# Two attention mixers of a decoder trunk: score products of two heads side by side, the causal mask on VectorE, another order at the seam between them, and output products moved ahead of a norm

## The chip, the cores and the metric

The kernel runs on one core of one Trainium2 chip. The metric is the device time of one execution in microseconds (us). The engines are TensorE (PE; PEld is its weight load), VectorE (DVE), ScalarE (ACT), GpSimd (POOL) and SyncE (SP, which issues most of the DMA). Each engine runs its own instructions in program order; semaphores tie the engines together.

## The reference, cut to what matters

The program computes two layers of a trunk with 512 positions and a width of 1024. In each layer one input projection feeds four token mixers, each 256 wide; one output product joins them, and a mixture of 32 experts follows.

```python
for l in range(DEPTH):                       # DEPTH = 2
    proj = rmsnorm(x, norm1_g[l]) @ w_in[l]
    pa, pb, pc, pd = jnp.split(proj, cut, axis=-1)
    out_a = moba_attention(...)              # 4 heads of 64, causal
    out_b = rwkv7_time_mix(pb, ...)          # linear recurrence, 4 heads of 64
    out_c = sgu_mix(...)                     # chunked gating
    out_d = diff_attention(...)              # 4 heads, two softmax maps of width 32 each
    mixed = jnp.concatenate([out_a, out_b, out_c, out_d], axis=-1)
    x = x + mixed @ w_out[l]
    x = x + hier_moe(rmsnorm(x, norm2_g[l]), ...)
return rmsnorm(x, final_g)

# in attention A, per head and block of 128 queries: s = q k^T, masked causally, then
p = jax.nn.softmax(s, axis=-1);  out = p @ v
# in attention D:
attn = p[:, :, 0] - lam * p[:, :, 1]         # of two softmax maps
o = rmsnorm(attn @ v, subln_g) * (1.0 - lambda_init)
```

With 512 positions every query block of A sees all past key blocks, so A is plain causal attention here. All numbers are 32-bit floats; each matrix product of the program leaves two MATMUL records in the trace, a transpose leaves one.

## The kernel before, in words

A layer has an input part (norm, projection), the mixers, the output product, the routing, and the expert part, where 32 experts' weights stream from HBM. The change is in the mixers and in the output product.

`mixer_steps()` writes out by hand the order of the mixers' steps; each engine runs the same list through `run_mixers` and skips what isn't its own. So an engine does its share of a step only after its share of all earlier steps. The steps that matter here:

- `("attn", (m, u))`, m = A or D: step u of an attention's pipeline over 16 units. A unit is one block of 128 queries of one head; A goes from the block with 1 key block (width 128) to the one with 4 (width 512), D from 512 down to 128. At step u PE makes the scores of unit u (L818, then L820, which adds the causal mask as a transposed product of a constant), transposes the probabilities of unit u-2 (L830), and multiplies those of unit u-3 with the values (L842). DVE takes the row maximum (L1538) of the scores in PSUM; for D it also joins the two maps (L1548, L1550, L1552). ACT copies the finished outputs of unit u-4 (L1222), then the transposed probabilities of unit u-2 (L1231), then takes the exponentials of unit u (L1239), in this order. L842 writes one bank only, so it waits for ACT's copy of the unit before (L1222). A head of A has 64 channels, a map of a head of D has 32: scores of neighbouring heads (A) or of the two maps (D) take different rows of the array. The scores rotate through four PSUM banks (3, 4, 5, 6).
- `("rwkv", (c, m, step))`: the recurrence in four chunks, for two pairs of heads c. Each chunk has parts Z (L733, L735), B (L741) and S (L748 to L758), each waiting on copies by ACT or DVE of the part before; chunk 3 leaves out L748 and L749. These parts are put between the attention units of A, by the table `UNITS_PER_PART`. F1, F2 and F3 (L762, L765, L770) and G (DVE only, L1525 and L1526) are the norm and gate behind it; they stand between steps of D.
- `("turn_qk", "D")` (L799): turns queries and keys of D; it stands near the end of A.
- `turns(j)` (L848) turns the outputs of A and of the gating mixer; `early_out` (L867) starts the output product of the first column half for two row blocks out of them, before D is done.

After the last step of D, PE makes four more output products each for row blocks 2 and 3 (L916), then waits for `mixed_done`: DVE squares, sums and scales D's outputs (L1561 to L1571) behind the last unit of D. Then PE turns D's outputs (L848) and the recurrence's scales (L898), and goes through the rest of the products, first column half, then second (L916). SP's queue holds loads of expert weights that wait for marks in this order: parts B and S of chunk 3, `mixed_done`, the output sums.

## Time and profile before

| | us |
|---|---|
| median of 3 runs | 1835.2 (1834.05 to 1835.56) |
| the profiled execution's own time | 1835.94 |
| its span, from first to last instruction | 1834.1 |
| mean granted TensorE clock | 0.962 |

| engine | busy us | share of the span |
|---|---|---|
| PE | 1622.2 | 88% |
| DVE | 576.0 | 31% |
| ACT | 286.3 | 16% |
| POOL | 158.9 | 9% |

The mixers with attention stand twice in the span, from about 237 to 352 us and from about 1140 to 1255 us; the output product follows each. From about 450 to 860 us and again in the second half the DMA engines are over 90% busy with expert weights. A row of the timeline gives the start, the length, the engine, line, operation and tile, the count of records it merges, and in brackets how long the engine was idle before it and what released it. Records of PE overlap, so the time that a group of products takes is read from its start to the next group's start. PEclk is the granted TensorE clock, where 1.00 is 2.4 GHz and 0.50 is 1.2 GHz.

### The profile page before, as it was taken

The page shows a single profiled execution, that of the slowest core. Times are in us where ns is not written, and L with a number is a line of the kernel's source. Part 1 is how long each engine was busy: PE and PEld are TensorE (multiplying, and loading weights), DVE is VectorE, ACT ScalarE, POOL GpSimd, SP SyncE. Part 2 cuts the span into 40 slices and gives each one's busy share as a digit, 9 for nine tenths or more (in the row PEclk, how much of TensorE's full clock was granted, in tenths as well). Part 3 has the DMA queues.
Part 4 walks back from the last instruction along what each step waited for, and adds up shares of the span by engine and source line. Part 5 has one row for each costly group of instructions (what it writes and reads, how often), then busy time and mean ns, then how long its engine had stood idle before and what let it go on. Part 6 is the DMA issues. An engine that isn't in the chain of part 4 may idle for free.

```text
span 1834.1 us, 22309 instructions
## 1 busy us (share of the span) xinstructions
PE 1622.2 (88%) x9240; PEld 989.8 (54%) x9240; DVE 576.0 (31%) x1282; ACT 286.3 (16%) x694; POOL 158.9 (9%) x175
## 2 busy tenths in 40 slices
PE   7999999998999788787799999989989987888773
PEld 3445776657565455444444557755665654545441
DVE  2174324625221111221422742264342211112115
ACT  3131144311000000000123212442200000000001
POOL 0010000002211011110000100000022111011000
PEclk9999997899999999999899999979999999999997
DMA  9212013149999999999821111214489999999994
GB/s 321 92 44 66 1 47 138 39 181 363 412 425 422 424 424 424 423 423 421 362 107 76 52 58 46 79 60 166 166 360 420 424 423 424 424 424 422 423 418 188
DMA packets 72712, 486.58 MB, mean 265 GB/s; under 512 B 24413, under 2 KB 26397, under 8 KB 37792
## 3 DMA queue, kind: packets, MB, share of 16 engines
q1 hardware_dynamic: 62240, 468.81, 62.3%
q0 software_dynamic: 10368, 16.30, 2.4%
q8 instruction: 76, 1.25, 0.3%
q14 instruction: 28, 0.23, 0.0%
HBM read 472.24 MB, written 30.21 MB: 274 GB/s over the span
## 4 chain that ended last, share of the span: by engine, by line
PE 62%; DMA 25%; DVE 5%; SPq 4%; issue 3%; ACT 1%; POOL 1%; DVEq 0%; POOLq 0%; ACTq 0%
PE banks L963 12%; PE banks L623 12%; DMA RING<-in_w_up 7%; PE banks L978 6%; PE banks L612 6%; DMA RING<-in_w_down 5%; PE banks L916 5%; DMA TOK<-in_w_up 4%; DMA RING<-in_w_gate 3%; PE banks L818 3%; DMA TOK<-in_w_gate 2%; PE banks L842 2%; SPq L493 2%; PE banks L941 2%; SPq L495 2%
## 5 line engine op out<-in xcount | busy, mean ns | idle before, releaser
L963 PE MATMUL banks<-RING,XS 128*64 128x256 f32 x2752 | 320.2, 389 | 50.2 <-DMA RING<-in_w_up 28.4
L963 PEld LDWEIGHTS banks<-RING,XS 128*64 128x64 f32 x2752 | 224.2, 140 | 157.3 <-issue 46.0
L623 PE MATMUL banks<-RING,XNT 128*128 128x512 f32 x512 | 224.3, 595 | 0.6 <-DMA RING<-in_w_in_blocks 0.6
L978 PE MATMUL banks<-RING,XS 128*64 128x512 f32 x768 | 178.8, 606 | 28.5 <-issue 15.5
L1794 DVE SCALAR_TENSOR_TENSOR XS<-banks,TABLE,XS 128x256 f32<-128x256 f32 x58 | 28.1, 484 | 447.0 <-PE banks L963 447.0
L623 PEld LDWEIGHTS banks<-RING,XNT 128*128 128x128 f32 x512 | 96.7, 191 | 117.9 <-issue 116.7
L1272 ACT ACTIVATE XS<-banks,TABLE 128x256 f32<-128x256 f32 x58 | 27.5, 474 | 791.6 <-PE banks L963 791.6
L978 PEld LDWEIGHTS banks<-RING,XS 128*64 128x64 f32 x768 | 61.6, 138 | 112.5 <-issue 112.5
L2012 POOL DMA_INDIRECT y_rows<-XS,SOLVE x64 | 64.5, 1007 | 543.0 <-DVE XS L1836 520.6
L612 PE MATMUL banks<-XNT,RING 128*128 128x512 f32 x256 | 110.2, 592 | 0.0
L1836 DVE COPY XS<-banks 128x512 f32<-128x512 f32 x64 | 44.3, 691 | 204.8 <-PE banks L978 192.0
L963 PE MATMUL banks<-TOK,XS 128*64 128x256 f32 x832 | 94.4, 380 | 13.0 <-DMA TOK<-in_w_gate 7.0
L916 PE MATMUL banks<-RING 128*128 128x512 f32 x224 | 100.2, 601 | 0.1
L963 PEld LDWEIGHTS banks<-TOK,XS 128*64 128x64 f32 x832 | 67.4, 137 | 43.6 <-issue 11.5
L612 PEld LDWEIGHTS banks<-XNT,RING 128*128 128x128 f32 x256 | 48.6, 190 | 61.2 <-issue 61.2
L1538 DVE TENSOR_REDUCE SMALL<-banks 128x1 f32<-128x128 f32 (+3 forms) x96 | 44.2, 488 | 107.8 <-PE banks L820 107.4
L916 PEld LDWEIGHTS banks<-RING 128*128 128x128 f32 x224 | 42.0, 193 | 48.0 <-issue 47.7
L818 PE MATMUL banks<-XNT 32*128 32x512 f32 (+7 forms) x192 | 61.5, 590 | 0.0
L842 PE MATMUL banks<-TOK,RING 128*128 128x64 f32 x320 | 51.3, 300 | 8.9 <-ACT TOK L1222 8.7
L842 PEld LDWEIGHTS banks<-TOK,RING 128*128 128x128 f32 x320 | 48.5, 223 | 14.0 <-issue 13.6
L969 PE MATMUL banks<-CF,XS 128*128 128x128 f32 x132 | 30.1, 310 | 25.6 <-DVE XS L1794 18.4
L1239 ACT ACTIVATE XNT<-banks,SMALL 128x128 f32<-128x128 f32 (+3 forms) x96 | 49.8, 526 | 14.0 <-DVE SMALL L1538 13.7
(335 smaller groups left out, 1783.7 us busy)
## 6 DMA issues: line engine op xcount, KB each, us to landing
RING<-in_w_down SPq DMA_DIRECT2D x46, 2048.0 KB, 27.0
RING<-in_w_up SPq DMA_DIRECT2D x44, 2048.0 KB, 28.4
RING<-in_w_gate SPq DMA_DIRECT2D x42, 2048.0 KB, 26.7
RING<-in_w_in_blocks SPq DMA_DIRECT2D x12, 2048.0 KB, 9.6
TOK<-in_w_gate SPq DMA_DIRECT2D x12, 2048.0 KB, 35.5
TOK<-in_w_up SPq DMA_DIRECT2D x10, 2048.0 KB, 32.4
XNT<-in_w_down SPq DMA_DIRECT2D x8, 2048.0 KB, 30.5
TOK<-in_w_down SPq DMA_DIRECT2D x6, 2048.0 KB, 30.9
```

Source lines behind the costliest of these rows:

```text
L493: sp.dma_start(dst, src.rearrange("a p n -> p (a n)")).then_inc(full, 16)
L612: last = mm(bank[:, :], w[:, k, j * P:(j + 1) * P], XNT[:, k, :], start=(k == 0), stop=(k == KD - 1))
L623: last = mm(bank[:, :], XNT[:, k, i * P:(i + 1) * P], w[:, k, :], start=(k == 0), stop=(k == KD - 1))
L818: mm(banks[a][:, 0:w], QKT[rows, h // 2, i * P:w], QKT[rows, 2 + h // 2, 0:w], start=True, stop=False)
L842: last = mm(PS[0][:, 0:HD], PT[:, n % 2, b * P:(b + 1) * P], VAD[:, b, v0:v0 + HD], start=(b == 0), stop=(b == i))
L916: last = mm(PS[SUM_BANK[n][i]][:, :], src[:, i * P:(i + 1) * P], w[:, k, :], start=(k == 0), stop=(k == (KD - 1 if n else 3)))
L963: last = mm(bank[f * CAP:(f + 1) * CAP, 0:256], rows[:, k, :], w[:, k, f * 256:(f + 1) * 256], start=(k == 0), stop=(k == KD - 1))
L978: last = mm(PS[5][n * CAP:(n + 1) * CAP, :], HT[:, j, f * CAP:(f + 1) * CAP], w[:, k, n * BN:(n + 1) * BN], start=(k == 0), stop=(k == KF ...
L1239: ac(PB[:, u % 2, a, 0:w], PS[SCORE_BANKS[k % 4]][:, 0:w], ACT.Exp, bias=nmx[:, base + n:base + n + 1], accum_out=sums[:, base + n:base + ...
L1538: V.tensor_reduce(nmx[:, base + n:base + n + 1], PS[SCORE_BANKS[k % 4]][:, 0:w], AX.X, ALU.max, negate=True).then_inc(s["maxed"], 1)
L1836: V.tensor_copy(YS[h], PS[5][:, :]).then_inc(y2_copied, 1)
L2012: pool.indirect_dma_start(y_halves, bass.IndirectOffsetOnAxis(ap=YROW[:, e:e + 1], axis=0), YS[h], None, bounds_check=4 * SEQ - 1, oob_is_ ...
```

## The change

Five things are edited, all within the mixers and the output product.

1. Scores of A are issued in pairs: at every even step PE issues those of two neighbouring heads behind each other (rows 0 to 63 and 64 to 127 of the array), at odd steps none. L820 goes for A; in its place DVE adds the mask to the block of the unit in PSUM, by one more instruction per unit ahead of the maximum, chained by a semaphore.
2. `UNITS_PER_PART` spreads the 16 units over the parts of chunks 0 to 2. Chunk 3 (Z, B, S) moves behind D's steps 0, 1 and 2. F1 and F2 stand one pair of heads at a time behind D's steps 3 to 6; F3 and G stand behind step 7 (before: 5 and 6); the four `turns` behind steps 7 and 8 (before: 9 and 11).
3. A's steps 17 and 18 now both stand ahead of D's step 0 (before: 17, D's 0, 18, 19).
4. `early_out` does one product at a time, behind D's steps 10 to 17 (before two at a time behind 14 to 17).
5. Four products of the second column half for row block 0 are made ahead of the wait for `mixed_done`, into bank 4. The recurrence's scales, turned into banks 4 and 7 before, go to banks 7 and 5; the second waits for DVE's first copy out of bank 5.

On PE at the start of attention A in layer 0, before (L799 turns A's queries and keys, L733 is Z, L741 is B of chunk 0):

```order
L799 MATMUL banks<-CF,TOK 128x128 x16
L733 MATMUL banks<-RING 128x64 x4
L818 MATMUL banks<-XNT 128x128
L820 MATMUL banks<-CF 128x128
L818 MATMUL banks<-XNT 128x128
L820 MATMUL banks<-CF 128x128
L741 MATMUL banks<-RING,X 128x64 x4
L818 MATMUL banks<-XNT 128x128
L820 MATMUL banks<-CF 128x128
L830 MATMUL banks<-CF,XNT 128x128
```

and after (L793, L727, L807, L735, L829 and L841 are the lines L799, L733, L818, L741, L830 and L842 of before):

```order
L793 MATMUL banks<-CF,TOK 128x128 x16
L727 MATMUL banks<-RING 128x64 x4
L807 MATMUL banks<-XNT 128x128 x2
L735 MATMUL banks<-RING,X 128x64 x4
L807 MATMUL banks<-XNT 128x128 x2
L829 MATMUL banks<-CF,XNT 128x128 x2
L841 MATMUL banks<-TOK,RING 128x64
```

Two scores stand in a row, and no mask product behind them.

On PE at the seam between the two attentions, before (L799 turns D's queries and keys; L818 and L820 are now D's scores and masks):

```order
L799 MATMUL banks<-CF,TOK 128x128 x16
L830 MATMUL banks<-CF,XNT 128x128 x4
L842 MATMUL banks<-TOK,RING 128x64 x4
L818 MATMUL banks<-XNT 128x512 x2
L820 MATMUL banks<-CF 128x128 x2
L842 MATMUL banks<-TOK,RING 128x64 x4
L818 MATMUL banks<-XNT 128x512 x2
L820 MATMUL banks<-CF 128x128 x2
L818 MATMUL banks<-XNT 128x512 x2
L820 MATMUL banks<-CF 128x128 x2
L830 MATMUL banks<-CF,XNT 128x128 x4
```

and after:

```order
L793 MATMUL banks<-CF,TOK 128x128 x16
L829 MATMUL banks<-CF,XNT 128x128 x4
L841 MATMUL banks<-TOK,RING 128x64 x8
L817 MATMUL banks<-XNT 128x512 x2
L819 MATMUL banks<-CF 128x128 x2
L727 MATMUL banks<-RING 128x64 x2
L729 MATMUL banks<-RING,SCAN 128x128
L727 MATMUL banks<-RING 128x64 x2
L729 MATMUL banks<-RING,SCAN 128x128
L817 MATMUL banks<-XNT 128x512 x2
L819 MATMUL banks<-CF 128x128 x2
L735 MATMUL banks<-RING,X 128x64 x4
```

A's last product with the values stands ahead of D's first scores, and Z and B of chunk 3 stand between D's scores.

On PE behind D's last unit, before:

```order
L842 MATMUL banks<-TOK,RING 128x64
L916 MATMUL banks<-RING 128x512 x8
L848 MATMUL banks<-CF,TOK 128x128 x8
L898 MATMUL banks<-CF,SCAN 128x128 x8
L916 MATMUL banks<-RING 128x512 x28
```

and after:

```order
L841 MATMUL banks<-TOK,RING 128x64
L917 MATMUL banks<-RING 128x512 x12
L847 MATMUL banks<-CF,TOK 128x128 x8
L899 MATMUL banks<-CF,SCAN 128x128 x8
L917 MATMUL banks<-RING 128x512 x24
```

Four of the output products (L916, L917) have moved ahead of the turns of D's outputs.

The diff, cut to its core:

```diff
-UNITS_PER_PART = [2, 1, 2, 1, 2, 2, 1, 2, 2, 1, 1]
+UNITS_PER_PART = [2, 2, 1, 2, 2, 2, 2, 2, 1]
...
-            for ch in range(4):
+            for ch in range(3):
                 for n, part in enumerate("ZBS"):
                     yield from both(part, ch)
...
-            second = ([("attn", ("A", 16)), ("turn_qk", "D"), ("attn", ("A", 17)), ("attn", ("D", 0)), ("attn", ("A", 18)), ("attn", ("A", 19))])
+            yield from [("attn", ("A", 16)), ("turn_qk", "D"), ("attn", ("A", 17)), ("attn", ("A", 18)), ("attn", ("D", 0))]
+            yield from both("Z", 3)
+            yield "attn", ("A", 19)
+            one = lambda c, *step: [("rwkv", (c, SCANS[c][1], step))]
+            beside = {1: both("B", 3), 2: both("S", 3), 3: one(0, "F", 1), 4: one(1, "F", 1), 5: one(0, "F", 2), 6: one(1, "F", 2),
+                      7: both("F", 3) + both("G") + [("turns", (0,))], 8: [("turns", (j,)) for j in range(1, 4)]}
+            for n, step in enumerate((i, k) for i in range(2) for k in (0, 1, 4, 5)):
+                beside[10 + n] = [("early_out", step)]
             for u in range(1, 20):
                 yield "attn", ("D", u)
...
+                yield from beside.get(u, [])
...
+                        if u < 16 and m == "A" and u % 2 == 0:
+                            i, h = unit_of[m][u]
+                            w = (i + 1) * P
+                            for a in range(2):
+                                k = 4 + u + a
+                                wait_bank(k)
+                                rows = slice(a * 64, a * 64 + 64)
+                                mm(score_bank(k)[:, 0:w], QKT[rows, h // 2, i * P:w], QKT[rows, 2 + h // 2, 0:w], start=True, stop=True).then_inc(s["scores"], 1)
+                        elif u < 16 and m == "D":
...
-                    for n, ks in ((0, (0, 1, 4, 5)), (0, (6, 7)), (0, (2, 3)), (1, range(KD))):
+                    early, late = (0, 1, 4, 5), (2, 3, 6, 7)
+                    for n, ks in ((0, early), (1, early), (0, (6, 7)), (0, (2, 3)), (1, range(KD))):
...
+                                if c:
+                                    pe.wait_ge(*at(layer, mt_v, 1))
                                 for ch in range(4):
-                                    last = tr(PS[(4, 7)[c]][:, ch * P:(ch + 1) * P], FIN[c][1][:, ch * P:(ch + 1) * P], ident)
+                                    last = tr(PS[(7, 5)[c]][:, ch * P:(ch + 1) * P], FIN[c][1][:, ch * P:(ch + 1) * P], ident)
...
-                        for i in (2, 3) if n == 0 and ks[0] == 0 else range(NT):
+                        for i in ((2, 3), (0,))[n] if ks is early else range(NT):
...
-                            for k in ks:
+                            for k in late if n and i == 0 and ks is not early else ks:
...
+                                if m == "A":
+                                    own = PS[SCORE_BANKS[k % 4]][:, i * P:w]
+                                    link(V.scalar_tensor_tensor(own, later, NEG, own, ALU.mult, ALU.add))
```

## Rows read from the trace of the kernel before

**Rows 1.** Windows: A and D of layer 0, D of layer 1, a stretch behind it.

```profile
core 0: us, PE busy (x) PEld busy (x) DVE busy (x) ACT busy (x) POOL busy (x), PEclk, DMA share, GB/s
237.20:287.12 49.92, 48.99 (x355) 37.53 (x353) 14.41 (x50) 27.08 (x85) 1.87 (x3) 1.00 0.22 85
287.12:351.98 64.86, 61.25 (x281) 40.06 (x281) 36.64 (x94) 30.46 (x103) 0.00 (x0) 0.74 0.14 59
1189.56:1254.85 65.29, 58.99 (x281) 38.67 (x281) 36.54 (x94) 30.77 (x103) 0.00 (x0) 0.79 0.14 59
1264.15:1270.00 5.85, 5.85 (x22) 3.83 (x23) 4.44 (x8) 0.00 (x0) 0.00 (x0) 0.71 0.80 308
```

**Rows 2.** Timeline of PE: a score of width 128, then A's step 15.

```profile
238.20 0.48 PE L818 MATMUL banks<-XNT 64*128 64x128 f32 x2
238.62 0.33 PE L820 MATMUL banks<-CF 128*128 128x128 f32 x1
...
275.89 1.12 PE L818 MATMUL banks<-XNT 64*128 64x512 f32 x2
276.95 0.33 PE L820 MATMUL banks<-CF 128*128 128x128 f32 x1
277.11 0.60 PE L830 MATMUL banks<-CF,XNT 128*128 128x128 f32 x4
277.55 1.00 PE L842 MATMUL banks<-TOK,RING 128*128 128x64 f32 x8
278.39 1.06 PE L741 MATMUL banks<-RING,X 128*128 128x64 f32 x8
```

**Rows 3.** Products on changing rows of the array: D's first scores, then the chunks' products.

```profile
287.12 1.13 PE L818 MATMUL banks<-XNT 32*128 32x512 f32 x4
...
L678 PE MATMUL banks<-SCAN x32: 376/376/480, 131.2 to 140.1; 64*128 64x256 f32 x32
```

**Rows 4.** DVE and ACT, groups by form: a 128x128 operation on PSUM, and what ends a unit.

```profile
L1456 DVE SCALAR_TENSOR_TENSOR TOK<-banks,PCOL,TOK 128x128 f32<-128x128 f32 x8 | 2.8, 351 | 3.0 <-PE banks L656 2.8
L1538 DVE TENSOR_REDUCE SMALL<-banks 128x1 f32<-128x512 f32 x12 | 7.9, 688 | 21.9 <-PE banks L820 21.9
L1239 ACT ACTIVATE XNT<-banks,SMALL 128x512 f32<-128x512 f32 x12 | 8.2, 684 | 5.6 <-DVE SMALL L1538 5.6
L1222 ACT ACTIVATE TOK<-banks,SMALL 128x64 f32<-128x64 f32 x32 | 10.1, 316 | 3.7 <-PE banks L842 3.7
```

**Rows 5.** Timeline of PE at the seam, layer 0.

```profile
282.14 1.07 PE L842 MATMUL banks<-TOK,RING 128*128 128x64 f32 x8 [0.23 <-ACT TOK L1222]
286.11 1.08 PE L842 MATMUL banks<-TOK,RING 128*128 128x64 f32 x8 [0.70 <-ACT TOK L1222]
291.06 1.94 PE L842 MATMUL banks<-TOK,RING 128*128 128x64 f32 x8 [2.45 <-ACT TOK L1222]
```

**Rows 6.** Windows over part Z and parts B, S of chunk 3, layer 0.

```profile
274.41:275.89 1.48, 1.48 (x14) 1.36 (x13) 0.00 (x0) 1.13 (x4) 0.00 (x0) 1.00 0.00 0
278.39:281.31 2.92, 2.92 (x30) 2.38 (x30) 0.65 (x3) 0.90 (x3) 0.00 (x0) 1.00 0.22 43
```

**Rows 7.** Windows where the clock falls or rises in D of layer 0.

```profile
288.00:290.00 2.00, 0.61 (x4) 0.20 (x2) 1.29 (x2) 0.73 (x3) 0.00 (x0) 0.81 0.97 418
...
306.00:308.00 2.00, 2.00 (x8) 0.58 (x7) 1.92 (x4) 0.63 (x1) 0.00 (x0) 0.92 0.00 0
316.00:318.00 2.00, 2.00 (x10) 0.91 (x10) 0.17 (x1) 0.00 (x0) 0.00 (x0) 0.64 0.00 0
332.00:334.00 2.00, 2.00 (x11) 1.70 (x12) 0.00 (x0) 1.15 (x4) 0.00 (x0) 0.59 0.00 0
```

**Rows 8.** Timelines of layer 1 around G: one of its four on DVE, then PE.

```profile
1223.10 0.75 DVE L1525 SCALAR_TENSOR_TENSOR RING<-RING,PCOL,XS 128x512 f32<-128x512 f32 x1
...
1226.78 0.55 PE L830 MATMUL banks<-CF,XNT 128*128 128x128 f32 x3 [2.83 <-DVE XNT L1552]
```

**Rows 9.** Timeline of PE behind D, layer 0.

```profile
351.98 7.09 PE L916 MATMUL banks<-RING 128*128 128x512 f32 x16
361.29 1.09 PE L848 MATMUL banks<-CF,TOK 128*128 128x128 f32 x8 [2.22 <-DVEq L1572]
```

More of the change, by code:

```diff
@@ L333, in mixer_steps @@
             first = [("attn", ("A", u)) for u in range(16)]
[L334 removed]
+            for ch in range(3):
                 for n, part in enumerate("ZBS"):
                     yield from both(part, ch)
[L337 to L343 removed]
+                    for _ in range(UNITS_PER_PART[3 * ch + n]):
+                        yield first.pop(0)
+            yield from [("attn", ("A", 16)), ("turn_qk", "D"), ("attn", ("A", 17)), ("attn", ("A", 18)), ("attn", ("D", 0))]
[6 more added lines that the diff above has]
+                beside[10 + n] = [("early_out", step)]
             for u in range(1, 20):
                 yield "attn", ("D", u)
[L346 to L355 removed]
+                yield from beside.get(u, [])
         def run_mixers(**do):
@@ L859, in turns, with early_out @@
                         turn_outputs(j, 1 + j % 2, src, t)
-                    def early_out(i, part):
-                        if part == 0:
+                    def early_out(i, k):
+                        if k == 0:
                             pe.wait_ge(*at(layer, mt_a, 4))
@@ L916, in _ @@
                                 last = mm(PS[SUM_BANK[n][i]][:, :], src[:, i * P:(i + 1) * P], w[:, k, :], start=(k == 0), stop=(k == (KD - 1 if n else 3)))
-                            if ks[-1] == (KD - 1 if n else 3):
+                            if ks is not early and ks[-1] == (KD - 1 if n else 3):
                                 last.then_inc(res_ps, 1)
@@ L1526, in rwkv @@
                             link(V.scalar_tensor_tensor(FIN[c][0], FIN[c][0], pc("lnb", c), gate, ALU.add, ALU.mult))
+                    later = CFs[:, CF["unit"][0]:CF["unit"][0] + P]
                     def attn(m, u):
```

31 lines of the change are left out of this document (5 added, 26 removed).

## The prediction

> **What bounds the kernel now.** I read the windows over the two attentions first, because every edit lies between 237 and 364 us of layer 0 and between 1140 and 1267 us of layer 1. In A (49.92 us in layer 0; layer 1 runs the same instructions and I take it as equal) PE is busy 48.99 us at a clock of 1.00, ACT 27.1 and DVE 14.4: PE bounds it, and what leaves PE shortens it [rows 1]. In D (64.86 and 65.29 us) PE is busy 61.25 and 58.99 us, but at a mean clock of 0.74 and 0.79, so about half of the time runs at 1.2 GHz; DVE is busy 36.6 us, ACT 30.5 [rows 1]. The timeline of PE gives the idle places: 0.23, 0.70 and 2.45 us at the seam, each ended by ACT's copy of outputs [rows 5], 2.83 us behind G in layer 1 [rows 8], and 2.22 us ahead of D's turned outputs [rows 9]. The windows of two microseconds show the clock falling at 289 us, behind the last of the seam's waits, and at 316 us, and coming back at 306 and 332 us [rows 7]. All of this is PE or what PE waits for. The DMA is busy 0.14 of D [rows 1]: the expert weights are loaded when marks of the mixers and of the output product are reached, so I take a shift of the mixers' end to arrive whole at the end of the span.
>
> **Part 1, pairs in A.** A single score of 64 rows takes 0.42 us from its start to L820's at width 128 and 1.06 at width 512 [rows 2]; 0.63 and 0.84 for the widths between are my estimate from the straight line. Do two on different rows run together? Both maps of D's first unit, four records of width 512, take 1.13 us with their end, the two records of one head of A 1.12 [rows 3, 2]. And 64 records of 64x256, L678 and L679 on alternating halves, of which the row of L678 stands for half, fill 131.2 to about 140.4 us: 0.144 us for one, against 0.31 by A's 0.63 for two [rows 3]. So a pair costs as much as one. Of four heads at each width two disappear: 2 x (0.42 + 0.63 + 0.84 + 1.06) = 5.9 us. L820 costs 0.16 us to the next start [rows 2], 16 times that 2.6. Together PE loses 8.5 us per layer. DVE gets 16 mask instructions of 0.35 us [rows 4], 5.6 us onto 14.4 in 50: hidden as a sum, but it lengthens the chain behind each score. At width 512 that chain is mask 0.35, maximum 0.69, exponential 0.68, output copy 0.32 [rows 4] and four handovers that I take at 0.1: 2.4 us until L842 of the next step may start. Between them PE has only some 1.7 us (turn 0.44, values 0.84, turn 0.44 [rows 2]) where an even and the following odd step stand together. The new table puts a chunk's part there in most places; where it doesn't or where the part is short (steps 2 and 3, 5, 7, 13) I count 0.8, 0.7, 0.2 and 0.2, so 1.9 us per layer. Bounds: 0, and 8 pairs x 1.2 = 9.6 us. I take 1.9 since PE waits nowhere in A now except at its end.
>
> The Trainium skill, TensorEngine Tiling (Array Packing), section Performance Considerations, warns that tiling speeds up TensorE but not the evacuation of PSUM, which may then bound. By this rule the paired stage would run at its readers' pace; it is the rival called readers below.
>
> **Part 2, the seam and chunk 3.** Z, B and S of chunk 3 (1.48 + 2.92 = 4.4 us [rows 6]) leave A and enter D. A's last product, 0.84 us [rows 2], now precedes D's scores. The 2.45 us wait came from ACT's order: the copy that frees L842's bank stood behind D's first two exponentials, and these behind scores and maxima. With A's step 18 ahead of D's step 0 it stands behind one copy; 0.5 us are left, somewhat more than L1222's own 0.32 [rows 4, 5]. The waits of 0.23 and 0.70 stay, the first growing to 0.7, because S no longer stands ahead of step 16. In D's steps 0 to 2 the chunk's parts lie where PE otherwise had only scores; for DVE's queue there I count 0.5 us. The parts B and S also release SP's reload of x and two weight loads later; the queue behind them is idle for tens of microseconds, so nothing.
>
> A, start to D's first score: 49.92 - 8.5 - 4.4 + 0.84 - 0.93 (idle of before) + 0.7 + 0.7 + 0.5 + 1.9 = 40.7 us, a gain of 9.2.
>
> **Part 3, D.** At full clock D's PE work is its busy time less half of what ran at 1.2 GHz. Layer 0: 64.86 x 0.26 x 2 = 33.7 us slow, 1.4 of them idle, so 61.25 - 16.2 = 45.1. Layer 1: 65.29 x 0.21 x 2 = 27.4, so 58.99 - 13.7 = 45.3 [rows 1]. After: 45.2 - 0.84 + 4.4 = 48.8 us. Waits: DVE piles up at F1 (about 2 us of DVE beside each of steps 3 and 4, with maxima and joining of about 2.6 against PE's 3.5): 1.6 us in sum over steps 4 to 6. Turns and G: G is four DVE instructions of 0.75 [rows 8], now directly behind F3. `turns` 3 waits for ACT's copy of `turns` 1, which stands in ACT's queue behind the exponentials of unit 8, which wait for maxima queued behind G: 3.1 + 0.4 + 1.1 + 0.6 = 5.2 us against 3.2 us of PE work in between, so 2.0 us, in place of the 2.83 that layer 1 had [rows 8]. First wait on F3's last DVE step: 0.4. With the 0.5 of part 2 that is 4.5. D without any slow clock: 53.3 us.
>
> **Part 4, the clock.** Before, it cost 16.2 and 13.7 us of PE's work (part 3). It fell behind the 2.45 us wait, behind the thin products of F3 in layer 0, behind the 2.83 us wait in layer 1, and each time stayed low for 13 to 17 us, until L762, a dense product of all rows, or L848 came [rows 7]. After, the first wait is gone, but F3 and the 2 us at `turns` 3 follow each other closely, so I expect a fall there in both layers, ended earlier because `early_out` (dense, full rows) starts at step 10: some 7 us low, 3 us lost. A fall at the seam remains possible in about one of three layers, at 6 us. Taken: 5 us per layer; bounds 0 and 16. D is then 58.3 us, a gain of 6.6 and 7.0.
>
> **Part 5, output products ahead of the norm.** PE works 7.09 us after its last unit and waits 2.22 [rows 9]. Four products are 8 records of 7.09 / 16 = 0.44: 3.5 us. They cover the 2.22 and are taken from later, where PE has no idle time; the gain is 2.22 per layer, and D's outputs are turned 1.3 us later relative to DVE, which the products behind them (7.1 us ahead of the first use of the recurrence's part) hide. The new wait on DVE's first copy ends when PE has turned the first scales, 1.3 us after the start: 0 to 0.3 us, taken 0, since the second copy is waited for anyway. In layer 1 the clock fell behind this wait: mean 0.71 over 5.85 us [rows 1], 5.85 x 0.29 = 1.7 us. Sum 2.2 x 2 + 1.7 = 6.1 us.
>
> **Sum.** 2 x 9.2 + 6.6 + 7.0 + 6.1 = 38.1 us. The profiled execution took 1835.9 us, 0.7 above the median; 1835.9 - 38.1 = 1797.8, or 1797 on the scale of the median.
>
> **Rivals.**
> - *No falls of the clock in D.* The seam's long wait is gone, and chunk 3 fills D's start. Against it: F3 and the wait at `turns` 3. 2 x 5 less: 1787 us.
> - *The clock is low as long as before.* D's scores, turns and narrow products kept it low for 13 to 17 us even with PE 100% busy [rows 7]; one fall at the seam and one at F3 give it again. 15 us per layer instead of 5, of which some 3 per layer return because waits on DVE and ACT disappear at half speed: + 14, 1811 us.
> - *Readers.* ACT and DVE set the pace of A: 9.6 instead of 1.9 us of waits per layer, + 15: 1812 us. Against it speak ACT's 27 and DVE's 20 us under PE's 37. The rule of the Trainium skill named above would have it so; the sums say no, the local chains partly yes.
> - *Pairs don't run together.* 5.9 us per layer stay on PE, of which it hides the 1.9 of waits: + 8, 1805 us. Against it: rows 3.
> - *Slower.* A now runs at 1.00 throughout because it has no gaps. With waits in it and less PE work the clock could fall early and stay down, as it did in D with PE 100% busy. 37 us of A's work at 1.2 GHz cost 37 less 3.8 of waits, 33 per layer: 1797 + 66 = 1863 us. It outweighs the gain once more than about 19 us of A's work per layer, half of it, run at half clock.
>
> **How the numbers follow.** Forecast 0.50, no falls 0.18, clock as before 0.17, readers 0.07, pairs 0.03, slower 0.03, and 0.02 for something that leaves the time as it is. The forecast case alone spans clock costs of 2 to 9 us and other waits of +-3 us per layer: 1785 to 1811. The range takes in the no-falls case with a few microseconds fewer waits, 1779, and the middle cases up to 1815. A measurement of this kernel can tell about 0.2% from no change. Faster by more than that 0.95, within it 0.02, slower 0.03.
>
> **What would show it.** In the profile after: A from its first score part to D's first score 40 to 42 us at clock 1.00; two L807 per pair in the time of one; PE's wait ahead of D's step 0 under 1 us; a wait of about 2 us ahead of the last three turns (L847), at D's step 8, with the clock falling near it; no wait ahead of D's turned outputs; D 54 to 63 us. The forecast is wrong if the clock in A is under 1.00, if waits in A sum to over 5 us, or if the weights' loads start no earlier although the mixers end earlier.

## The result and the profile after

The changed kernel takes 1824.4 us (median of 14 executions, 1809.1 to 1836.7) against 1834.7 us (14 executions, 1829.4 to 1844.9) of the kernel before on the same chip. The ratio is 0.993 (95%: 0.991 to 0.9951), some 13 us faster. The forecast was 1797 us, with 1815 as the upper end: the sign was right, the size was not. A ratio is formed without executions over 1.5% above the fastest of their kernel, so it can stand below the ratio of the medians (by the medians the change is worth 10 us, and the ratio given for e1 rests on two of its six executions).

The changed kernel was measured twice more without any edit: e1 was profiled in one of its longest executions, e13 in its shortest. Together with the first they are the key to this case, so all three are read here. First, the page of the changed kernel (span, busy time of PE, then busy tenths and granted clock in 40 slices of the span):

```profile
span 1811.6 us, 22279 instructions
...
PE 1602.1 (88%) x9208; PEld 978.8 (54%) x9208; DVE 583.2 (32%) x1314; ACT 286.3 (16%) x694; POOL 158.8 (9%) x175
...
PE   7999999999799888777799999999998997988773
...
PEclk9999997999999999999999999979999999999997
```

This profiled execution took 1813.4 us, 11 below the median. The only slices with a clock under nine tenths, apart from the last, are those of D in layer 0 and layer 1. The windows over A (from its first score part to D's first score) and D (from there to the first output product behind it), layer 0 and then layer 1; columns as in [rows 1]:

```profile
237.22:281.14 43.92, 39.09 (x306) 31.07 (x304) 17.80 (x64) 26.22 (x82) 1.86 (x3) 0.99 0.09 38
281.14:344.87 63.73, 62.37 (x314) 40.03 (x313) 36.95 (x96) 31.35 (x106) 0.00 (x0) 0.79 0.25 99
1129.90:1175.23 45.33, 40.66 (x307) 32.63 (x305) 17.80 (x64) 26.54 (x82) 1.86 (x3) 0.95 0.09 37
1175.23:1239.04 63.81, 62.50 (x314) 40.07 (x313) 36.95 (x96) 31.40 (x106) 0.00 (x0) 0.79 0.26 99
```

Against [rows 1], A has lost 6.0 and 4.6 us and D only 1.1 and 1.5. The clock of D is 0.79, where the forecast had it low for some 7 us. A isn't at 1.00 in either layer, which the prediction had named as a sign of being wrong: the clock is low for its last microsecond, and in layer 1 also for 3.4 us from 1167.6 us.

The timeline of PE shows that the pairs run as meant (L807), and which waits A now has (L841 is the product with the values, L1223 ACT's copy of its outputs, L793 the turning of D's queries and keys):

```profile
238.23 0.49 PE L807 MATMUL banks<-XNT 64*128 64x128 f32 x4
238.65 1.10 PE L735 MATMUL banks<-RING,X 128*128 128x64 f32 x8
...
261.52 1.13 PE L807 MATMUL banks<-XNT 64*128 64x512 f32 x4
...
271.62 1.08 PE L841 MATMUL banks<-TOK,RING 128*128 128x64 f32 x8 [0.23 <-ACT TOK L1223]
272.53 0.61 PE L829 MATMUL banks<-CF,XNT 128*128 128x128 f32 x4
274.14 1.08 PE L841 MATMUL banks<-TOK,RING 128*128 128x64 f32 x8 [1.00 <-ACT TOK L1223]
...
278.11 1.08 PE L841 MATMUL banks<-TOK,RING 128*128 128x64 f32 x8 [0.70 <-ACT TOK L1223]
279.68 1.53 PE L841 MATMUL banks<-TOK,RING 128*128 128x64 f32 x8 [0.50 <-ACT TOK L1223]
281.14 2.08 PE L817 MATMUL banks<-XNT 32*128 32x512 f32 x4
```

Two scores of width 512 take 1.13 us, where one took 1.12 [rows 2]. The wait of 2.45 us behind D's first scores [rows 5] is gone; A's last product with the values, now ahead of these scores, waits 0.50 us. The last row is the point of this document: D's first scores take 2.08 us, against 1.13 in [rows 3]. The clock has fallen at the seam all the same, without the long wait. It fell at 280.1 us, within the last L841, which is why that row takes 1.53 us where the others take 1.08.

Now e13, the same program, in the same four stretches:

```profile
237.22:280.68 43.46, 38.64 (x306) 30.66 (x304) 17.80 (x64) 26.20 (x82) 1.86 (x3) 1.00 0.09 39
280.68:336.13 55.45, 53.41 (x313) 34.63 (x313) 36.76 (x96) 31.15 (x106) 0.00 (x0) 0.94 0.30 114
1120.62:1164.63 44.01, 39.19 (x307) 31.15 (x305) 17.80 (x64) 26.20 (x82) 1.86 (x3) 0.99 0.09 39
1164.63:1226.97 62.34, 60.48 (x313) 38.92 (x313) 36.88 (x96) 31.34 (x106) 0.00 (x0) 0.82 0.27 102
```

And the same stretch of its PE:

```profile
278.11 1.08 PE L841 MATMUL banks<-TOK,RING 128*128 128x64 f32 x8 [0.70 <-ACT TOK L1223]
279.68 1.08 PE L841 MATMUL banks<-TOK,RING 128*128 128x64 f32 x8 [0.50 <-ACT TOK L1223]
280.68 1.13 PE L817 MATMUL banks<-XNT 32*128 32x512 f32 x4
```

The rows ahead of the seam agree with those above to 0.01 us, waits included; in one execution the last L841 takes 1.53 us, in the other 1.08. And e1, the first 58 us of D in both layers:

```profile
281.36:339.36 58.00, 57.65 (x206) 37.92 (x207) 26.82 (x58) 20.44 (x59) 0.00 (x0) 0.50 0.28 109
1185.96:1243.96 58.00, 57.65 (x206) 37.92 (x207) 26.83 (x58) 20.44 (x59) 0.00 (x0) 0.50 0.28 109
```

PE is busy 57.65 of 58 us, and runs at 1.2 GHz throughout. The lengths of A and D account for the whole difference between the executions of the changed kernel:

| trace | A, layers 0 and 1 | D, layers 0 and 1 | sum | its execution |
|---|---|---|---|---|
| before | 49.92, 49.92 | 64.86, 65.29 | 230.0 | 1835.9 |
| changed | 43.92, 45.33 | 63.73, 63.81 | 216.8 | 1813.4 |
| changed, e1 | 43.45, 43.46 | 76.86, 76.83 | 240.6 | 1836.6 |
| changed, e13 | 43.46, 44.01 | 55.45, 62.34 | 205.3 | 1801.9 |
| forecast | 40.7, 40.7 | 58.3, 58.3 | 198.0 | 1797.8 |

From the second row to the third the sum rises by 23.8 us and the time by 23.2; to the fourth it falls by 11.5 and the time by 11.5. The changed kernel's time varies with that of D, and D's with the time for which the clock stays low.

Between the profiled executions of before and after lie 22.5 us: 13.2 from A and D, 6.2 from part 5 (below), and 3.1 from elsewhere; outside the mixers the clock of this execution was low for some 41 us in sum, before for 51.

### The profile page after: what moved, and what is told of

The parts are those of the page before. It is cut to its first block, busy times and chain, and to the rows that moved or that the text cites. A ratio compares the mean times of both kernels' runs of the same rounds, so it can differ in the third digit from the quotient of the medians.

```text
span 1811.6 us, 22279 instructions
## 1 busy us (share of the span) xinstructions
PE 1602.1 (88%) x9208; PEld 978.8 (54%) x9208; DVE 583.2 (32%) x1314; ACT 286.3 (16%) x694; POOL 158.8 (9%) x175
## 4 chain that ended last, share of the span: by engine, by line
PE 62%; DMA 26%; DVE 4%; issue 3%; SPq 3%; ACT 1%; POOL 1%; DVEq 0%; POOLq 0%; ACTq 0%
PE banks L617 12%; PE banks L964 11%; PE banks L606 6%; DMA TOK<-in_w_up 6%; PE banks L979 6%; PE banks L917 5%; DMA RING<-in_w_up 5%; DMA RING<-in_w_gate 3%; DMA RING<-in_w_down 3%; DMA TOK<-in_w_gate 2%; DMA SCAN<-in_w_up 2%; PE banks L841 2%; SPq L487 2%; PE banks L942 2%; PE banks L817 2%
## 5 line engine op out<-in xcount | busy, mean ns | idle before, releaser
L964 PEld LDWEIGHTS banks<-RING,XS 128*64 128x64 f32 x2752 | 220.8, 139 | 157.9 <-issue 43.1
L979 PEld LDWEIGHTS banks<-RING,XS 128*64 128x64 f32 x768 | 61.1, 138 | 111.6 <-issue 111.6
L917 PE MATMUL banks<-RING 128*128 128x512 f32 x224 | 99.1, 595 | 0.0
L917 PEld LDWEIGHTS banks<-RING 128*128 128x128 f32 x224 | 41.5, 190 | 47.1 <-issue 46.9
L841 PE MATMUL banks<-TOK,RING 128*128 128x64 f32 x320 | 48.7, 287 | 9.8 <-ACT TOK L1223 9.4
L841 PEld LDWEIGHTS banks<-TOK,RING 128*128 128x128 f32 x320 | 44.7, 207 | 16.3 <-issue 15.1
L1136 ACT ACTIVATE TOK<-banks 128x512 f32<-128x512 f32 x32 | 19.2, 599 | 203.8 <-PE banks L617 203.8
L1986 POOL DMA_INDIRECT XS<-x_rows,SOLVE x32 | 33.8, 1058 | 191.6 <-PE banks L957 189.3
```

Source lines behind the costliest of these rows:

```text
L841: last = mm(PS[0][:, 0:HD], PT[:, n % 2, b * P:(b + 1) * P], VAD[:, b, v0:v0 + HD], start=(b == 0), stop=(b == i))
L917: last = mm(PS[SUM_BANK[n][i]][:, :], src[:, i * P:(i + 1) * P], w[:, k, :], start=(k == 0), stop=(k == (KD - 1 if n else 3)))
L964: last = mm(bank[f * CAP:(f + 1) * CAP, 0:256], rows[:, k, :], w[:, k, f * 256:(f + 1) * 256], start=(k == 0), stop=(k == KD - 1))
L979: last = mm(PS[5][n * CAP:(n + 1) * CAP, :], HT[:, j, f * CAP:(f + 1) * CAP], w[:, k, n * BN:(n + 1) * BN], start=(k == 0), stop=(k == KF ...
```

## The experiments

**Where the loss is: e1, the changed kernel again (no edit).**

> The changed kernel once more, unchanged, for a second trace and for the spread of its times. Theory 'clock': the changed kernel's time differs between executions by how much of it runs at 1.2 GHz; over the executions the time falls as the mean granted clock rises, by about 1.5 to 2 us for each 0.001 of the clock, and a trace of a slower execution (over 1820 us) shows low stretches inside attention A that the first trace (1813 us) has only in layer 1. Rival 'loads': the spread comes from the expert weights' loads; then the mixers of a slower execution take what those of the first trace take (A 43.9 and 45.3 us, D 63.7 and 63.8 us) and the difference lies between 450 and 860 us or behind 1380 us.

Measured: 1834.4 us (1805.7 to 1839.1, 6 executions), ratio 0.9881 (0.982 to 0.9941); the kernel before beside it has the same median, 1834.2. The mean clock of an execution goes with its time: 0.966 at 1805.7 us, 0.949 at 1836.6. The trace is the one shown above: low at the seam, and low for 58 us. The loads are not the cause, as A and D hold the whole difference to the first trace. But the low stretches were expected inside A, and there the clock is 1.00 in both layers: they lie in D.

**The waits at the seam filled: e2.** Five dense products of all rows, 256 wide, stand where PE waits in A's steps 16 to 18. Nothing reads what they write.

```diff
+                    def fill(n):
+                        for _ in range(n):
+                            mm(PS[1][:, 0:2 * P], cst("head"), CFs[:, CF["unit"][0]:CF["unit"][0] + 2 * P], start=True, stop=True)
...
+                        if m == "A" and u in {16: 2, 17: 2, 18: 1}:
+                            if u == 16:
+                                pe.wait_ge(*at(layer, mix["A"]["s_done"], 3))
+                            fill({16: 2, 17: 2, 18: 1}[u])
```

> The changed kernel with five dense products of width 256 on all rows (constants, results unused, about 0.44 us each) put into PE's three waits at the seam: two ahead of the value products of A's step 16, two at step 17, one at step 18. Theory 'clock': the fall at the seam, 23 to 24 us low in both layers, is what ate the gain; with the waits filled the clock stays at 1.00 through D's first steps in at least one layer, D shrinks from 63.7 to some 52 us there, and the time falls by 8 to 20 us against the changed kernel. Rival 'narrow products': the clock falls because of what PE computes at the seam and in D's start (32 rows, turns, narrow products), not because of the waits; then it falls a few microseconds later anyway and the time stays within 4 us of the changed kernel's.

Measured: 1807.2 us (1797.5 to 1814.4, 6), ratio 0.9838 (0.9799 to 0.9877), the kernel before on that chip 1834.2. Added work makes the kernel some 15 us faster: it is 27 below the kernel before, where the changed kernel was 10 and 13 below in its two larger sets of executions. A is as long as before the edit, 43.47 us. The timeline of PE in e2 (L798 fills, L821 is D's score, L849 the product with the values):

```profile
278.42 1.07 PE L849 MATMUL banks<-TOK,RING 128*128 128x64 f32 x8
279.33 0.65 PE L798 MATMUL banks<-CF 128*128 128x256 f32 x2
279.99 1.08 PE L849 MATMUL banks<-TOK,RING 128*128 128x64 f32 x8
281.00 1.13 PE L821 MATMUL banks<-XNT 32*128 32x512 f32 x4
...
296.92 1.38 PE L849 MATMUL banks<-TOK,RING 128*128 128x64 f32 x8 [1.27 <-ACT TOK L1231]
298.09 2.02 PE L756 MATMUL banks<-RING,CF 128*128 128x512 f32 x2
```

The seam is crossed at 1.00 in both layers. The clock falls later in layer 0, behind the wait of 1.27 us at D's step 4, and stays low for 30.7 us; in layer 1 behind F3, for 17 us. D is 66.1 and 60.2 us, not the 52 that were expected for one of them: there are two more places where the clock falls. At the seam itself the count is clear. Over all traces, two layers each, the clock fell at 16 of 18 seams whose waits are open (the changed kernel, e3, e4, e8, e9, e12, e14) and at none of 10 with the five products in them (e2, e6, e7, e10, e11). The five end the waits and make the stretch denser at the same time, and no run parts the two.

**Both filled: e6**, e2 with eleven such products ahead of D's scores at steps 1 to 9:

```diff
+                                if a == 0:
+                                    fill({1: 1, 2: 1, 3: 1, 4: 2, 5: 1, 6: 2, 7: 1, 8: 1, 9: 1}.get(u, 0), banks[0])
```

> The changed kernel with the five dense products at the seam and eleven more in D (width 256, all rows, about 0.44 us each), ahead of the scores of D's units 1 to 9, written into the bank that the scores overwrite. Theory 'clock': D's own products, of 32 rows or 64 columns, let the clock fall at the next wait and do not bring it back; with dense products between them low stretches in D are 3 to 7 us long instead of 24 to 58 in both layers. D costs 4.8 us more of PE work, of which its waits take 2, and takes 54 to 60 us; time 1788 to 1803 us, 20 to 35 below the changed kernel, and a spread under 12 us. Rival: low stretches don't get shorter, and the kernel is 5 us slower than the one with the seam filled (1807).

Measured: 1799.8 us (1797.2 to 1802.0, 4), ratio 0.9778 (0.9743 to 0.9813). D 58.8 and 60.1 us with 6.8 and 10.2 us at 1.2 GHz, about what the forecast had (58.3, with 7). The spread is 5 us over four executions, against over 30 for the changed kernel.

**D alone filled: e8**, the changed kernel with the eleven of D only.

> The changed kernel with the eleven dense products in D alone; the three waits at the seam stay. Theory 'clock': the fall at the seam (280 us) still comes, but is over within 4 to 14 us instead of 24 to 58, as dense products come at D's steps 1, 2 and 3; time 1800 to 1815. Rival 'waits alone': what matters is the wait at the seam, and the low stretch stays 24 us or longer: 1825 us or more.

Measured: 1808.2 us (1799.8 to 1816.8, 4), ratio 0.9814 (0.9756 to 0.9871). The profiled execution is the longest of the four: D 65.5 and 66.6 us, the clock falls at the seam as before and stays low for 17.1 us, not for the 4 to 14 that were expected. In this trace products put into D don't prevent the fall; the stretch is shorter than the 24 and 58 us of the first trace and e1, and as long as e13's of layer 1.

**Few products where the waits are: e11**, e2 with six in D, at steps 4, 5, 8 and 9:

```diff
+                                if a == 0:
+                                    fill({4: 2, 5: 1, 8: 2, 9: 1}.get(u, 0), banks[0])
```

> The changed kernel with the five dense products at the seam and six in D, only where PE waits or makes thin products: two at D's step 4, one at 5, two at 8, one at 9. Theory 'clock': the falls come from the wait of 1.28 us at step 4 and from F3 with the wait behind it; products there do what eleven do at half the cost: D 55 to 58 us, 1792 to 1802 us. Rival: D's own narrow products between them suffice for a fall, some execution has a stretch over 15 us in D, and the time is 1803 to 1812.

Measured: 1796.4 us (1795.1 to 1799.2, 4), ratio 0.9812 (0.9789 to 0.9835), the kernel before on that chip 1829.6. It has the lowest median of this study, with every execution below the shortest of the changed kernel; by its ratio it can't be told from e6. Its windows over A and D:

```profile
237.97:281.44 43.47, 40.70 (x317) 32.20 (x315) 17.80 (x64) 26.20 (x82) 1.86 (x3) 1.00 0.09 39
281.44:338.37 56.93, 55.94 (x325) 36.72 (x325) 36.85 (x96) 31.15 (x106) 0.00 (x0) 0.94 0.29 112
1122.67:1166.14 43.47, 40.70 (x316) 32.19 (x315) 17.80 (x64) 26.21 (x82) 1.87 (x3) 1.00 0.09 39
1166.14:1223.20 57.06, 56.06 (x325) 36.65 (x325) 36.86 (x96) 31.15 (x106) 0.00 (x0) 0.94 0.28 111
```

Against the changed kernel's trace the sum of the four falls by 15.9 us and the execution by 15.9 (1797.6 against 1813.4).

**What brings the clock back: e9 and e14**, the changed kernel with F1 and F2 of both pairs of heads in a row:

```diff
-            beside = {1: both("B", 3), 2: both("S", 3), 3: one(0, "F", 1), 4: one(1, "F", 1), 5: one(0, "F", 2), 6: one(1, "F", 2),
+            beside = {1: both("B", 3), 2: both("S", 3), 3: both("F", 1), 5: both("F", 2),
```

> The changed kernel with F1 and F2 for both pairs of heads in a row again (F1 behind D's step 3, F2 behind step 5), as in the kernel before; everything else as changed. In the trace of a slow execution of the changed kernel one fall at the seam lasted 58 us, over both single F1 and both single F2; in the kernel before every fall at the seam ended within 17 us, at the two F1 in a row. Theory 'split': the change split the dense products that brought the clock back, and this is what makes the long stretches; with F1 together none at the seam lasts over 24 us, D takes 60 to 65 us, the times lie at 1805 to 1820 us with no execution over 1825. Rival 'seam only': the stretches of 58 us still occur, and the times spread up to 1830 us and over as with the changed kernel.

Measured: 1811.7 us (1807.2 to 1815.0, 4), ratio 0.9897 (0.9868 to 0.9926). The seam falls, 23.9 us low as in the changed kernel's first trace, but no execution is a long one, as expected. Four executions are few, so this and the changed kernel ran again beside each other, for one question: do single F1 and F2 make the long executions?

> The changed kernel unchanged, beside the kernel with F1 and F2 together, on one chip. Theory 'split': its times spread over 1806 to 1838 us as in the 20 executions so far, median 1820 to 1832, and more than half of them are over 1820 us. Rival 'chance or chip': on this chip it lies at 1807 to 1818 like the kernel with F1 and F2 together.

> The changed kernel with F1 and F2 for both pairs of heads in a row, once more. Theory 'split': 1805 to 1820 us in all executions, median at least 8 us below the changed kernel's on the same chip. Rival: same spread as the changed kernel, medians within 5 us.

Measured: changed kernel 1823.2 us (1801.9 to 1835.9, 10), ratio 0.9929 (0.9898 to 0.996); with F1 and F2 together 1811.9 (1805.4 to 1826.8, 6), ratio 0.9877 (0.9838 to 0.9916). Taken together, 10 of 30 executions of the changed kernel took over 1830 us, and none of 10 with the heads together; the medians over all are 1824.6 and 1811.9. The trace of e1 shows how: it has a single F1 at 302.77 us as the first trace has one at 302.55. First the changed kernel's trace, then that of e1:

```profile
302.55 1.81 PE L756 MATMUL banks<-RING,CF 128*128 128x512 f32 x2
304.30 0.91 PE L817 MATMUL banks<-XNT 32*128 32x384 f32 x4
```

```profile
302.77 2.02 PE L756 MATMUL banks<-RING,CF 128*128 128x512 f32 x2
304.72 1.65 PE L817 MATMUL banks<-XNT 32*128 32x384 f32 x4
```

The scores behind F1 take 0.91 us in the one and 1.65 in the other: with one pair of heads the return at this place is a matter of the execution. e1's stretch ended at 339.4 us, behind twelve turns in a row (L847). That splitting makes the long executions is supported by the counts and not shown: side by side on one chip it is 2 of 10 against 0 of 6, the intervals of the two ratios overlap, and two executions of e14 (1820.8 and 1826.8 us) lie above the 1820 that were expected as its upper end.

**e10, e2 and e9 together.**

> As the one before, and the five dense products in the waits at the seam. Theory 'split': the seam doesn't fall, and a later fall ends sooner: 1790 to 1805 us. Rival: the two F1 in a row make DVE late (4 us of its work in one step), PE waits 1 to 3 us at step 4 or 5, the clock falls there and the time is that of the seam filled alone (1807) or more.

Measured: 1802.5 us (1798.3 to 1804.3, 4), ratio 0.9841 (0.9816 to 0.9867), D 60.3 and 57.6 us. It lies below e2 and spreads less, but lies above e11: with both F1 ahead of step 4 the wait there is 2.14 us instead of 1.27, and the clock falls 1.5 us into it, for 10.2 us.

**What the pairs are worth: e3, e7, e5, e12.** e3 is the changed kernel with A's scores single and the mask on PE again:

```diff
-                        if u < 16 and m == "A" and u % 2 == 0:
-                            i, h = unit_of[m][u]
-                            w = (i + 1) * P
-                            for a in range(2):
-                                k = 4 + u + a
-                                wait_bank(k)
-                                rows = slice(a * 64, a * 64 + 64)
-                                mm(score_bank(k)[:, 0:w], QKT[rows, h // 2, i * P:w], QKT[rows, 2 + h // 2, 0:w], start=True, stop=True).then_inc(s["scores"], 1)
-                        elif u < 16 and m == "D":
+                        if u < 16:
...
-                                if m == "A":
-                                    own = PS[SCORE_BANKS[k % 4]][:, i * P:w]
-                                    link(V.scalar_tensor_tensor(own, later, NEG, own, ALU.mult, ALU.add))
```

> The changed kernel with its new step order, seam and output products, but A's scores one head at a time with the mask added on PE, as before. Prediction's term: PE loses 8.5 us per layer by the pairs and gets back 1.9 in waits, so this should be 2 x 6.6 = 13 us slower than the changed kernel. Theory 'clock': the unpaired A has no waits and keeps a clock of 1.00 in every execution, so this kernel is only 0 to 8 us slower than the changed one and its times spread less (under 10 us between the fastest and the slowest, against 28).

Measured: 1817.3 us (1808.2 to 1818.9, 6), ratio 0.989 (0.9857 to 0.9924); A 47.85 and 47.33 us, D 63.7 and 61.3. The prediction's terms had this kernel 13 us slower than the changed one, the theory of the clock 0 to 8. Neither came: its median is 7 us shorter, though by the ratios the two can't be told apart, and its times spread by 11 us. e7 asks the same with the clock held up (e6 without pairs):

> As the one with all sixteen dense products, but A's scores one head at a time and the mask on PE as before. With the clock held in both, the difference is the pairs' own worth. From the traces: A's PE work is 8.5 us more per layer, its waits 7 us less except the 3 at its end, so 4 to 5 us per layer, 8 to 10 us slower than with pairs. Rival (the prediction's number): 13 us slower. Rival 'pairs do harm': equal or faster.

Measured: 1808.5 us (1807.6 to 1821.2, 5), ratio 0.9829 (0.9795 to 0.9863), against 1799.8 of e6. A of layer 0 is 47.71 us against 43.45: pairs are worth 4.3 us per layer, and 8.7 in the median. A of layer 1 shows something else:

```profile
1127.70:1187.49 59.79, 59.78 (x332) 45.50 (x330) 14.00 (x48) 26.06 (x82) 1.86 (x3) 0.77 0.07 28
```

PE is busy 59.78 of 59.79 us, and the clock was low for 27.3 us of it, from 1131.9 us. This execution, 1821.2 us, is the only one of the five above 1808.7. In its layer 0 the clock fell nowhere in A or D. These are D's window and its longest wait there, ahead of the last four of the turns (L852 in this kernel):

```profile
285.82:342.58 56.76, 54.89 (x336) 35.69 (x335) 36.84 (x96) 31.04 (x106) 0.00 (x0) 1.00 0.29 112
322.48 0.65 PE L852 MATMUL banks<-CF,TOK 128*128 128x128 f32 x4 [1.05 <-ACT RING L1250]
```

e5 is the kernel before with the pairs and the mask on DVE alone, the edit of e3 the other way round.

> The kernel before with the pairs alone: A's scores two heads at a time, mask on VectorE; step order, seam, chunk 3 and output products as before. By the prediction's terms PE loses 8.5 us per layer; the old table has more adjacent steps, so waits of up to 4 us per layer come back: A 41 to 45 us instead of 49.9, D as before, 10 to 17 us faster than before. Theory 'clock' (the long low stretch in D, 24 to 58 us, ate the gain): the old order has its dense products F1 one step earlier and the 2.45 us wait at the seam as before, so the falls are those of before (17 us each) and the gain arrives: 8 to 17 us. Rival 'pairs do harm': with gaps in A the clock falls in A too and the kernel is within 5 us of before.

Measured: 1835.1 us (1824.5 to 1837.7, 10), ratio 0.9986 (0.9963 to 1.0008): nothing, where 8 to 17 us were expected. A is 2.4 us shorter per layer, and D 2.6 and 2.2 us longer: the low stretches in D are 17.1 and 23.9 us in both layers, where the trace of before has 17.1 and 17.1, then 13.7 and 13.7. In this trace D's clock took what A gave; A itself kept a clock of 1.00, so the rival's number came and its mechanism didn't.

e12 leaves out A's causal mask altogether, to price DVE's 16 instructions.

> The changed kernel with A's causal mask left out altogether (DVE's 16 instructions per layer; the output is that of an attention that also sees the later keys of its own block). From first score part to D's first score A takes 43.5 us at full clock with the mask. Theory 'chain': the 0.35 us mask and its handover lengthen the chain that ends PE's waits on ACT at A's odd steps; without it A takes 41.5 to 42.7 us. Rival: the waits come from ACT's own queue and A stays within 0.3 us of 43.5.

Measured: 1805.5 us in one execution; A 42.84 and 42.50 us instead of 43.5. In layer 0 the seam's fall lies in the last 0.8 us of A and costs 0.4 of it, so the mask lengthens A by some 1.0 us per layer, not by most of the 2.8 that A is over its forecast.

**The products ahead of the norm: e4**, the changed kernel without the four of the second column half:

```diff
-                    for n, ks in ((0, early), (1, early), (0, (6, 7)), (0, (2, 3)), (1, range(KD))):
+                    for n, ks in ((0, early), (0, (6, 7)), (0, (2, 3)), (1, range(KD))):
...
-                            for k in late if n and i == 0 and ks is not early else ks:
+                            for k in ks:
```

> The changed kernel without the four products of the second column half ahead of D's norm (they are made where they were before; the banks of the turned scales stay 7 and 5). Prediction's term: 2.2 us per layer and 1.7 for a fall of the clock in layer 1, so 4 to 6 us slower than the changed kernel. Rival: DVE's chain behind the turned outputs is late by the 1.3 us that PE works longer, and the gain is under 2 us.

Measured: 1830.7 us (1808.9 to 1845.0, 12), ratio 0.9948 (0.9918 to 0.9978); the interval overlaps that of the changed kernel, so the term is read from the traces. The wait is back, in the trace of e4 behind D of layer 0:

```profile
336.24 7.09 PE L917 MATMUL banks<-RING 128*128 128x512 f32 x16
345.54 1.09 PE L847 MATMUL banks<-CF,TOK 128*128 128x128 f32 x8 [2.22 <-DVEq L1578]
```

From D's end to the first product of L941 (L942 after), the next stage, it is 64.49 and 65.83 us in e4 and 64.49 and 65.84 in the kernel before, but 62.05 in both layers of the changed kernel: 2.44 and 3.8 us. In layer 0 of this trace the seam kept its clock, and D was 55.40 us with 6.8 us low, as in layer 0 of e13.

## Why the prediction was right or wrong

**Bound and shift: right.** PE and what it waits for set the time, and a shift of the mixers' end arrives whole at the end of the span; the table above closes to a microsecond over the three traces of the changed kernel, and leaves 3.1 us between before and after.

**Part 1, the pairs run together: right. Their waits: mis-sized.** A at full clock is 43.46 us, not 40.7. A (e13, layer 0) has ten listed waits, 4.8 us in sum where 3.8 were forecast, which explains 1.0. Each wait begins only when the products ahead of it have ended, some 0.16 us behind the moment at which the next could have started: ahead of the 1.00 us wait, L829 starts at 272.53 and ends at 273.14, while in e2, where a product follows, the next one starts 0.45 us behind it. A of before had two such waits, so eight more ends, about 1.3 us by this estimate, were left out of the sum. The remaining 0.5 us is not placed. So pairs are worth 4.3 us per layer (e7 against e6), not 8.5 - 1.9 = 6.6.

The waits are nearly all ended by ACT's copy of the outputs, so the rival "readers" had its mechanism right and its price too high: pairs cost 8.5 - 4.3 = 4.2 us of waits, not 9.6. TensorEngine Tiling (Array Packing) in the Trainium skill, Performance Considerations, says that tiling speeds up TensorE but not the evacuation of PSUM. By this rule the pairs would give way to their readers' pace, and the trace agrees in part: half of the 8.5 us that left PE came back as waits, though the readers are busy 26 and 18 of 43 us.

**Part 2, the seam: right in its rows.** The wait is 0.50 us as forecast, and 0.23, 1.00 and 0.70 ahead of it against 0.7 and 0.7, so 0.5 us more in sum. That the fall would go with the long wait was the reading that failed, below.

**Part 3, D's work and waits: right in sum, by two misses that cancel.** 53.3 us were forecast at full clock, some 53.1 come out of the traces. D's work is 50.0 us against 48.8: e13's layer 0 is busy 53.41 us with 6.8 low, and e7's layer 0 is busy 54.89 us with eleven added products of 0.44. The waits are some 3.1 us against 4.5: 2.0 in e13 (1.28 of them at step 4), where the turns ran at half clock and the wait at `turns` 3 is missing, and 1.05 for that wait at full clock in e7. The work may be short in part because the sum halved the slow time, while groups take less than double at half clock (below); this was not tested. The 53.1 is an estimate, up to 0.4 us too low, since one added product stands ahead of that wait in e7.

**Part 4, the clock: the step that failed.** Forecast: a fall at F3, some 7 us low, 3 lost, and one at the seam in one of three layers at 6 us; taken 5 us per layer, bounds 0 and 16. The fall at F3 came as forecast (6.8 us low from 310 us in e13, layer 0). That at the seam came in five of the six layers of the three traces of the changed kernel, and lasted 17 to 58 us instead of about 12. With the 58 us D is 76.9, 23.8 above the 53.1; in the first trace's layer 0, with 26 us of low clock in it, 63.7, 10.6 above. The median of all 30 executions, 1824.6 us, lies 11.2 above the first trace. If that is the mixers, and no fall reaches into A, D is about 70.5 us per layer and the clock costs some 17 us (an estimate), over three times the 5 that were taken and just above the upper bound of 16. Two readings were wrong in it. The 2.45 us wait was taken for the cause of the fall, and said to stand ahead of it [rows 5, 7]. In layer 0 of before it doesn't: PE is idle from 288.61 to 291.06 us, and the clock falls at 289.3, when 0.6 us of this wait are over (in layer 1 it falls 0.3 us behind the wait). Two windows of before split the wait of layer 0 where the clock falls:

```profile
288.61:289.25 0.64, 0.01 (x1) 0.00 (x0) 0.64 (x2) 0.00 (x0) 0.00 (x0) 1.00 0.95 410
289.25:291.06 1.81, 0.00 (x0) 0.03 (x1) 0.58 (x1) 1.65 (x5) 0.00 (x0) 0.50 1.01 434
```

Waits of 0.50 to 1.00 us among narrow products were enough in the changed kernel. And the length of a fall was read as 13 to 17 us from places where something soon ended it: in before the two falls at the seam ended within the four records of F1 (L762), the other two at the end of turns (L848). That the change splits F1 and moves it behind more narrow products was costed at nothing. What decides the length is open, beyond the counts of e9 and e14.

The sum with measured terms, against the first trace: 1797.8, + 5.5 for A's waits, + 2.4 where the clock was low in A, - 0.4 for D's work and waits, + 11.3 for D's clock (10.6 + 10.7 - 10), - 3.1 elsewhere: 1813.5, measured 1813.4. This closes by construction, since the 3.1 is what the windows leave. With e1's clock (23.8 + 23.7 - 10 = 37.5 instead of 11.3, and no fall in A) it is 1837.3, measured 1836.6, and that is a test.

**Part 5: right.** 2.44 and 3.8 us against 2.2 and 3.9.

**Rivals.** "The clock is low as long as before" (1811 us) is the nearest, and too mild for the median: in e1 the clock is low for 58 us of D in each layer, in the trace of before for 34 and 27, and in the changed kernel's first trace for some 26 in each. Its remark that waits disappear at half speed holds in part: the 26.3 us low in D of layer 0 should cost 13.2, and D is 10.6 longer; 58 should cost 29, and it is 23.8. The vanished waits are some 3 of that; besides, a group takes less than double at half clock (D's scores 2.08 us against 1.13). "Slower" was put into A; the same mechanism, low with PE 100% busy, sits in D instead (and in A of e7). Its reason, that A runs at 1.00 because it has no gaps, doesn't hold for e7: that A has none either, and its clock fell 6 us behind the last idle time of PE. "No falls" occurred in no trace of the changed kernel; layer 0 of e7 had none, with sixteen added products and no pairs.

What the forecast described exists: e11 has the clock it assumed, by six and five added products, and takes 1796.4 us. That this meets the forecast of 1797 so closely is luck: its A and D are 2.9 us longer in sum than forecast, and the rest is 3.1 us shorter.

## What to carry to other kernels

Where the granted clock falls, don't put it down to the longest wait ahead of it: look at everything that PE runs around it, and cost the stretch from what will bring the clock back, with a bound as long as the stage. When PE's work is thinned and its waits get shorter but more, take the time at either clock as two cases, profile several executions, and try dense products that nobody reads in the waits: here eleven per layer were worth some 20 us (e11 lies 33.3 us below the kernel before, the changed kernel on the same chip 13.1). A wait costs its listed idle time and the end of the product ahead of it, 0.16 us here, so many short waits are dearer than their sum.

## What the runs showed of the hardware that was not expected

- TensorE stayed at 1.2 GHz for 58 us with PE busy 57.65 of them, in both layers of e1; in the kernel before the longest such stretch in D was 17 us.
- In the kernel before the clock fell 0.6 us into a wait of 2.45 us (layer 0, at 289.3 us), not behind it.
- Two executions of one program, with the same rows and the same waits to 0.01 us ahead of the seam, got different clocks behind it (0.50 in one, 1.00 in the other; D 63.7 and 55.4 us). What decides between them isn't in these traces and stays open.
- In the one long execution of e7 the clock fell within A of layer 1 and stayed low for 27.3 us, with PE busy 59.78 of A's 59.79 us; PE had last been idle, for 0.84 us, until 1125.9 us, and the fall came at 1131.9.
- Two products on 64 rows each, issued behind each other on different halves of the array, take the time of one at widths 128 (0.42 us from start to next start for both) and 512 (1.13 us with the end).
- The kernel's mean clock and its time go together over nearly all executions of the changed kernel, from 0.969 at 1801.9 us to 0.945 at 1839.1.
